# Feed-forward opening, decay expansion and second-half product order of a hybrid decoder layer

## What is computed

```python
z = h @ w_in                                    # all head groups from one projection
log_a = log_sigmoid((a_low @ w_gate_up + b_gate)) / GLA_TAU      # a_low has 16 columns
y_gla = rms_norm(gla_chunked(q, k, v, log_a)) * silu(g)
y_conv = c_b * causal_short_conv(c_c * c_h, conv_w)
y_xa = memory_cross_attention(xq, mk, mv)
mix = concatenate([y_gla, y_conv, y_xa]) @ w_out
x = layer_norm(alpha * x + mix, ln1_g, ln1_b)
ff = square(relu(x @ w_ff1)) @ w_ff2            # 1024 -> 4096 -> 1024
x = layer_norm(alpha * x + ff, ln2_g, ln2_b)
```

## Time and profile before

| | |
|---|---|
| median of three runs | 2171.8 us (2170.22 to 2173.83) |
| the profiled execution | 2171.97 us, of which the span from the first to the last instruction is 2170.3 us |
| PE busy | 2082.6 us (96%) |
| DVE busy | 1389.6 us (64%) |
| ACT busy | 1006.3 us (46%) |
| POOL busy | 516.7 us (24%) |
| mean granted TensorE clock | 0.987 of 2.4 GHz |

### The profile page before, as it was taken

The page is one execution under the profiler, slowest core; times in us unless marked ns, Lnnn a source line. Parts: engine busy times, 40 slices in busy tenths (PEclk is TensorE's granted clock), DMA queues, the critical chain, the costliest instruction groups (busy, mean ns, idle before and its releaser), DMA issues.

```text
span 2170.3 us, 28904 instructions
## 1 busy us (share of the span) xinstructions
PE 2082.6 (96%) x11392; PEld 1685.1 (78%) x11392; DVE 1389.6 (64%) x1898; ACT 1006.3 (46%) x1344; POOL 516.7 (24%) x483
## 2 busy tenths in 40 slices
PE   7999999999999999799999999999999999999996
PEld 5677787778777777688888788888788888788884
DVE  3668566756765687656556776666665645954458
ACT  3535454444444445545445654544433333633334
POOL 3002001101110213011000244444684700810004
PEclk9999999999999999899999999999999999999998
DMA  6222333324242514255646778777968665665563
GB/s 196 59 59 88 107 95 121 107 78 143 72 127 59 175 53 134 87 189 196 221 153 218 270 256 285 248 272 271 333 203 284 196 193 187 222 224 194 193 194 136
DMA packets 241063, 374.26 MB, mean 172 GB/s; under 512 B 16368, under 2 KB 117776, under 8 KB 240928
## 3 DMA queue, kind: packets, MB, share of 16 engines
q1 hardware_dynamic: 212096, 272.68, 38.6%
q0 software_dynamic: 28832, 99.74, 13.3%
HBM read 272.74 MB, written 99.61 MB: 172 GB/s over the span
## 4 chain that ended last, share of the span: by engine, by line
PE 51%; DVE 6%; ACT 2%; DMA 2%; issue 1%; POOL 0%; SPq 0%; DVEq 0%; ACTq 0%; POOLq 0%
PE main L68 9%; PE main L70 9%; PE main L69 9%; PE sc L68 6%; PE sc L69 6%; PE sc L70 6%; DVE w_lo L1563 3%; PE aux L70 1%; PE ob L70 1%; PE ob L68 1%; PE aux L68 1%; PE ob L69 1%; PE aux L69 1%; DMA w_b<-in_w_ff_dram 1%; DMA x_piece<-normed_dram 1%
## 5 line engine op out<-in xcount | busy, mean ns | idle before, releaser
L1563 DVE TENSOR_TENSOR w_lo<-w_b,w_hi 128x1024 fp32r<-128x1024 f32 x144 | 217.5, 1513 | 241.5 <-ACT w_hi L1533 241.5
L1563 DVE TENSOR_TENSOR w_lo<-raw,w_hi 128x1024 fp32r<-128x1024 f32 x144 | 205.5, 1430 | 128.6 <-ACT w_hi L1533 128.6
L1533 ACT ACTIVATE w_hi<-raw 128x1024 fp32r<-128x1024 f32 x144 | 152.5, 1060 | 256.7 <-PE main L70 112.6
L1533 ACT ACTIVATE w_hi<-w_b 128x1024 fp32r<-128x1024 f32 x144 | 152.2, 1057 | 176.9 <-PE aux L70 81.3
L1053 DVE TENSOR_TENSOR w_lo<-raw,w_hi 128x1024 fp32r<-128x1024 f32 x116 | 140.9, 1222 | 140.4 <-ACT w_hi L763 139.6
L68 PE MATMUL main<-xT_lo,w_hi 128*128 128x512 f32 (+1 forms) x528 | 217.2, 411 | 1.5 <-DVE xT_lo L1065 1.5
L69 PE MATMUL main<-xT_hi,w_lo 128*128 128x512 f32 (+1 forms) x528 | 205.5, 389 | 0.0
L70 PE MATMUL main<-xT_hi,w_hi 128*128 128x512 f32 (+1 forms) x528 | 205.4, 389 | 0.0
L68 PE MATMUL sc<-x_lo,w_hi 128*128 128x512 f32 x448 | 175.6, 392 | 8.4 <-DVE x_lo L1506 6.1
L68 PE MATMUL main<-x_lo,w_hi 128*128 128x512 f32 x448 | 175.7, 392 | 8.0 <-ACT z L1884 8.0
L68 PE MATMUL main<-w_lo,w_hi 128*128 128x512 f32 x448 | 175.8, 392 | 5.1 <-DVE w_lo L1563 5.0
(11 more groups left out here) (254 smaller groups left out, 4664.7 us busy)
## 6 DMA issues: line engine op xcount, KB each, us to landing
raw<-in_w_in_dram SPq DMA_DIRECT2D x80, 512.0 KB, 3.7
h_dram<-z SPq DMA_DIRECT2D x64, 512.0 KB, 3.9
raw<-h_dram SPq DMA_DIRECT2D x112, 256.0 KB, 2.7
w_b<-h_dram SPq DMA_DIRECT2D x112, 256.0 KB, 2.7
h_dram<-h_s SPq DMA_DIRECT2D x48, 512.0 KB, 4.0
rows<-in_x_dram POOLq DMA_DIRECT2D x32, 512.0 KB, 4.9
raw<-in_w_out_dram SPq DMA_DIRECT2D x32, 512.0 KB, 3.7
raw<-in_w_ff_dram SPq DMA_DIRECT2D x32, 512.0 KB, 6.7
```

Source lines behind the costliest of these rows:

```text
L1533: act.activation(ff.w_hi[:, n % RING, :], slot_tile(ff, m), ACT.Copy).then_inc(ff.hi_done, 1)
L1563: dve.tensor_tensor(ff.w_lo[:, n % RING, :], slot_tile(ff, m), ff.w_hi[:, n % RING, :].bitcast(F32), ALU.subtract).then_inc(ff.lo_done, 1)
```

## The change

Five things change.

1. **Decay expansion.** The low-rank value has 96 rows (hi, lo of the weight, three times) and is kept in fp32r: ACT copies all 96, DVE then subtracts in rows 64 to 95 to get the low part there. `w_gate` holds the matching six copies of the 16 rows, one pair of them as a low part. The two matmuls a block are fp32r, 96 rows deep. At the start six copies of `w_gate_up` are loaded instead of two, and ACT and DVE prepare the tiles in eight small instructions instead of two.
2. **Opening.** `x_high` and `x_low` are split into part 0 (three raw quarters, ready with the evacuation) and part 1 (four sums). Two of the four emptying instructions of the left half move ahead of the split of slot 6, the other two behind the sums of step 3. The splits of step q follow its own sums at once. The first product waits for part 0 of step 7 only, and product 1 for part 1. Slot splits 0 and 1 move back behind steps 5 and 7. The transposes of step 8 move from chunk 0 to chunk 1.
3. **Chunk 0.** ACT normalises two row tiles between snapshots 0 and 1 and two between 1 and 2. The tiles `z22` and `z12` change places with `h_s1` and `h_s4`, so that the snapshots wait for no store; DVE waits for the stores before it writes `h_s1` and `h_s4`. DVE forms the sum for slot 4 before the statistics.
4. **Second half.** The sequence is 5, 0, 1, 2, 3, 4, 6, so tiles 0 to 3 are complete after product 3. Products 4 and 6 then use the same banks back to back: the last two slots of product 4 run tile by tile (`BY_TILE`), and each bank is emptied before product 6 starts on it. Tiles 0 to 3 are finished during product 4, entirely by DVE in two passes, `(x - mean) * gain` (1024 wide) and `* rstd + bias` (two of 512), with ACT computing rstd only. POOL only stores them.
5. **Tail.** The last eight slots run tile by tile; four of them are held in memory of `acc0`, which the first half no longer needs. Tiles 4 to 7 are finished one by one behind their matmuls in the same two passes and stored in halves of 512 columns.

The diff, cut to its core:

```diff
@@ tiles
-            ff.z22, ff.z12, ff.z21 = (expand_sb(name, [P, 2, 512]) for name in ("z22", "z12", "z21"))
+            ff.h_s4, ff.h_s1, ff.z21 = (expand_sb(name, [P, 2, 512]) for name in ("h_s4", "h_s1", "z21"))
...
-            ff.h_s1, ff.h_s2 = (expand_sb(name, [P, 2, 512]) for name in ("h_s1", "h_s2"))
+            ff.z22, ff.h_s2 = (expand_sb(name, [P, 2, 512]) for name in ("z22", "h_s2"))
...
-            ff.h_s4 = expand_sb("h_s4", [P, 2, 512])
+            ff.z12 = expand_sb("z12", [P, 2, 512])
...
-        low = sb("low", [P, KT, 2 * RANK], F32R)
-        w_gate = sb("w_gate", [2 * RANK, 256])
+        low = sb("low", [P, KT, 6 * RANK], F32R)
+        w_gate = sb("w_gate", [6 * RANK, 256], F32R)
@@ mixer: POOL, ACT and DVE
-                             (w_gate[0:RANK, :], w_gate_up[0]),
-                             (w_gate[RANK:2 * RANK, :], w_gate_up[0]),
+                             *((w_gate_raw[RANK * i:RANK * i + RANK, :], w_gate_up[0]) for i in range(6)),
...
-                act.activation(lowT, aux[0:2 * RANK, :], ACT.Copy).then_inc(aux_free, 1)
+                act.activation(lowT, aux[0:6 * RANK, :], ACT.Copy).then_inc(gate_hi, 1)
...
+                dve.wait_ge(gate_hi, t + 1)
+                dve.tensor_tensor(lowT[64:96, :], aux[64:96, :], lowT[64:96, :].bitcast(F32), ALU.subtract
+                                  ).then_inc(aux_free, 1)
@@ x_evacuate, x_high
-        act.wait_ge(ff.x_lo_done, q if q >= 7 else q - 1)
+        act.wait_ge(ff.x_lo_done, 2 * (q if q >= 7 else q - 1))
...
+    if part == 0:
+        act.wait_ge(ff.x_evac, 2 * q + 2)
+    else:
+        act.wait_ge(ff.x_sum, 4 * q + 4)
     if q >= 6:
-        act.wait_ge(ff.x_lo_done, 6)
+        act.wait_ge(ff.x_lo_done, 2 * 6)
@@ slots
+SEQUENCE = [[0, 1, 2, 3, 4, 5, 6], [5, 0, 1, 2, 3, 4, 6]]
+SAME_TILE = [{3: 2, 4: 1, 5: 0}, {0: 5, 3: 2, 4: 1}]
+BY_TILE = 2
 TAIL = 4
-TAIL_K = 3
+TAIL_K = 8
+LAST_HELD = 2 * CONTRACT_SLOTS - TAIL_K
...
+    elif s >= LAST_HELD + 4:
+        act.wait_ge(ff.slot_used, m - 7)
+    elif s >= LAST_HELD:
+        act.wait_ge(ff.out_stored[s - LAST_HELD], 16)
     else:
         act.wait_ge(ff.slot_used, m - 3)
@@ PE
                 if m == 0:
-                    pe.wait_ge(ff.x_lo_done, X_STEPS)
+                    pe.wait_ge(ff.x_lo_done, 2 * X_STEPS - 1)
+                elif m == 1:
+                    pe.wait_ge(ff.x_lo_done, 2 * X_STEPS)
...
+                    if hf == 1 and p == 6 and k == 0:
+                        pe.wait_ge(fo_free, 4 * place(hf, p) - 4 + t + 1)
                     ins = piece(hf, p, k, t)
@@ ACT
-            if chunk == 0:
-                if i > 0:
-                    act.wait_ge(ff.stored[i], 16 * (HALF_CHUNKS // 2))
-            else:
+            if chunk > 0:
...
+        def inverse_deviation(c):
+            act.wait_ge(ln_stats, NT + c + 1)
+            act.activation(rstd[:, c:c + 1], mvar[:, c, 1:2], ACT.Ln, bias=eps_ln[:, :]).then_inc(ln_step, 1)
+            act.wait_ge(ln_step, 3 * NT + 2 * c + 1)
+            act.activation(rstd[:, c:c + 1], rstd[:, c:c + 1], ACT.Exp, scale=-0.5).then_inc(ln_step, 1)
...
+            if hf == 1 and at == 5 and k in (1, 4, 7, 10):
+                inverse_deviation(k // 3)
@@ DVE
+            elif p in (1, 3):
+                dve.wait_ge(ff.stored[{1: 2, 3: 1}[p]], 16 * (HALF_CHUNKS // 2))
...
+        def centred(c, step):
+            dve.wait_ge(ln_stats, NT + c + 1)
+            dve.scalar_tensor_tensor(out=acc[1][:, c, :], in0=acc[1][:, c, :], scalar=nmean[:, c:c + 1],
+                                     in1=g2_row[:, :], op0=ALU.add, op1=ALU.mult).then_inc(step, 1)
+
+        def scaled(c, step, n, ready):
+            dve.wait_ge(step, n)
+            dve.wait_ge(ln_step, 3 * NT + 2 * c + 2)
+            for d in range(2):
+                cols = slice(512 * d, 512 * d + 512)
+                dve.scalar_tensor_tensor(out=acc[1][:, c, cols], in0=acc[1][:, c, cols], scalar=rstd[:, c:c + 1],
+                                         in1=b2_row[:, cols], op0=ALU.mult, op1=ALU.add).then_inc(ready, 1)
...
+            if hf == 1 and at == 5 and k == KF - BY_TILE:
+                for t in range(4):
+                    if t < 3:
+                        dve.wait_ge(by_tile, t + 1)
+                    else:
+                        dve.wait_ge(slot_used, product_done(1, 4))
+                    add(1, 4, t)
```

More of the change, by code:

```diff
@@ L997, in _ @@
             split(0, 3)
[L998 to L999 removed]
+            act.wait_ge(small_landed, 16 * 11)
+            for i in range(3):
+                act.activation(low[:, :, 2 * RANK * i:2 * RANK * i + RANK], low_raw, ACT.Copy).then_inc(low_hi_done, 1)
+            act.activation(w_gate[:, :], w_gate_raw, ACT.Copy).then_inc(low_hi_done, 1)
             for i in range(4):
@@ L1687, in _ @@
                     sp.wait_ge(h_stored[p], 16 * CHUNKS)
-            for p in range(PRODUCTS):
+            for p in SEQUENCE[hf]:
                 for k in range(KF):
@@ new lines, in scaled @@
+        def scaled(c, step, n, ready):
+            dve.wait_ge(step, n)
+            dve.wait_ge(ln_step, 3 * NT + 2 * c + 2)
+            for d in range(2):
+                cols = slice(512 * d, 512 * d + 512)
+                dve.scalar_tensor_tensor(out=acc[1][:, c, cols], in0=acc[1][:, c, cols], scalar=rstd[:, c:c + 1],
+                                         in1=b2_row[:, cols], op0=ALU.mult, op1=ALU.add).then_inc(ready, 1)
+        for s in range(2 * CONTRACT_SLOTS):
+            hf, at, k = s // CONTRACT_SLOTS, s // KF % PRODUCTS, s % KF
+            if k == 0 and s > 0 and not (hf == 1 and at == 6):
+                h0, p0 = (hf, SEQUENCE[hf][at - 1]) if at else (hf - 1, SEQUENCE[hf - 1][6])
+                dve.wait_ge(slot_used, product_done(h0, p0))
+                for t in range(4):
+                    add(h0, p0, t)
+            if hf == 1 and at == 5 and k == KF - BY_TILE:
+                for t in range(4):
+                    if t < 3:
+                        dve.wait_ge(by_tile, t + 1)
+                    else:
+                        dve.wait_ge(slot_used, product_done(1, 4))
+                    add(1, 4, t)
+            if s + 4 < 2 * CONTRACT_SLOTS:
+                slot_low(dve, ff, EXPAND_SLOTS + s + 4)
+            if hf == 1 and at == 0 and 2 <= k < 10:
+                statistics(0, k - 2, 28)
+            if hf == 1 and at == 5 and 1 <= k < 13:
+                c = (k - 1) // 3
+                if k % 3 == 1:
+                    statistics(1, c, 48)
+                elif k % 3 == 2:
+                    if c == 0:
+                        dve.wait_ge(row_landed, 16 * 4)
+                    centred(c, head_step)
+                else:
+                    scaled(c, head_step, c + 1, head_ready)
+            if hf == 1 and at == 6 and k < 4:
+                half_statistics(1, TAIL + k, 1, 52)
```

292 lines of the change are left out of this document (161 added, 131 removed).

## The result

The changed kernel takes 2128.3 us (median of four runs, 2126.3 to 2131.0) against 2172.5 us for the kernel before on the same chip, 44 us less by the medians. Forecast were 2135.0 us, a gain of 37 us, in a range of 2128 to 2146 us, so the direction was right and the median lies just inside the range. The same kernel was timed once more later, beside other runs of before, and gave 0.9837 (0.9824 to 0.9851): 35 us by the ratio, 36.6 us by the medians. The profiled execution has a span of 2127.7 us where before had 2170.3 us, 42.6 us less.

A forecast was written before the change was run, and what follows sets the result against it. PE, busy for 96% of the span, was taken to bound the kernel. Gains of 19 + 8 - 0.5 + 3.5 + 7.1 = 37.1 us off 2171.97 us gave 2135 us, range 2128 to 2146 us for 8 in 10.

The forecast's parts named there:

- Opening: Up to product 4 of chunk 0: PE's waits go or shrink, 19 us gained, bounds 12 and 23.5 us.
- Forecast waits of 2.5 and 0.7 us: Chunk 0, before products 3 and 4: PE still waits 2.5 and 0.7 us for snapshots 1 and 2.
- allowance: Up to product 4 of chunk 0: 19 us taken instead of 20.4 us, for semaphores or a slower clock.
- waits found again between 930 and 1030 us: Sign of being wrong: the same waits a chunk later, where six steps of x operands fall in three chunks.
- Decay: Eight decay matmuls in the mixer: 1.02 us saved on each, 8 us taken, bounds 5.4 and 8.2 us.
- start-up: Start of the kernel: more DMA issues and small instructions for the decay tiles cost 0.5 us, bounds 0 and 2 us.
- Second half: From product 4 of the second half to the last slot: net gain 3.5 us, bounds 0 and 5.4 us.
- both terms: Last products of the second half: 5.4 us of wait and clock gained, 1.9 us lost to a new wait.
- the new wait: Before product 6's first matmul in the second half: PE waits about 2 us because DVE reaches the four adds late.
- End: Behind the last matmul: 7.5 us instead of 14.6 us, gain 7.1 us, bounds 6 and 8 us.

The follow-up runs named there:

- The additional run: The changed kernel with the last four slots by tile instead of eight (TAIL_K = 4); ratio to the kernel before 0.9846 (0.9831 to 0.9860).

## Why the prediction was right

- **Opening: right, and its marks hold.** No wait at the right-hand pieces. The stretch from the start of the projection to the first product was counted as 882.5 - 831.7 = 50.8 us and took 51.1 us. Forecast waits of 2.5 and 0.7 us before products 3 and 4 came out as 1.86 and 0.19 us. The count by hand gave 20.4 us; taking 19 for allowance was the only error, 1.8 us. Two steps in it were judged wrongly in their weight: letting the first product go with part 0 alone is worth nothing once the row tiles are next (run with the coarser wait, in which the splits themselves stay in two parts), and moving step 8, which got no term, guards some 4 us of the gain (4.87 us wait without it). One of the prediction's signs of being wrong, waits found again between 930 and 1030 us, did show in small: the waits for row pieces, 1.03 and 0.58 us before, are 2.69 us at 966.43 us and 1.09 us at 1007.62 us.
- **Decay: right.** 1.01 us a matmul by the starts (660.96 to 662.67 us before, and 652.49 to 653.19 us after, 1.71 less 0.70), so 8.1 us; with start-up 7.5 us between the means of all mixers. The Trainium skill (FP8 and Floating Point Precision, TensorE Precision Notes) has four passes for a true fp32 matmul, which would save 0.68 us each; the rows have 1.01 us, so by them the old one held PE for 0.23 + 1.01 = 1.24 us. The 10.6 us of the one pair hold 3 us of chance.
- **Second half: the net, 3.7 for 3.5 us, was right by luck, since both terms were too small.** The prediction took DVE's first addition, 2106.91 us, for the end of product 5. PE's first matmul of product 6 starts at 2104.42 us; the addition stood behind a slot split. So product 6 took 51.1 us and lost 7.6 us, not 5.4. On the other side the new wait was 1.90 us as forecast, with groups of 9.2 us (9.3 forecast), but it came at the last two slots of product 4, for a slot split, not before product 6 for the emptied bank, and in this profile cost 1.6 us more by the clock, which six of the seven other profiles with this wait don't show. 7.6 less 1.9 and 1.6 is 4.1; 3.7 was measured. In the later run of the same kernel the stretch takes 310.4 us: 5.3 us gained.
- **End: right.** 7.51 us from the start of the last matmul, 7.5 forecast; the gain is 7.5 and not 7.1 us because the prediction counted the 14.6 us of before from DVE's addition and not from the matmul (14.97 us). The additional run shows why: 4.53 us of DVE a tile must fit into the PE time of a tile.
- **What no term held:** 2.8 us lost in the expansion and 2.7 us won at the start of the contraction. The loss is no chance: it is in all nine profiles that have both the new mixer and the whole new opening, and in none of the four without one of the two. PE's waits for row pieces, which grew from 1.6 to 3.8 us, make up 2 us of it; they are 3.5 to 3.8 us in those nine, 1.8 us with the opening alone and 2.1 us with the mixer alone. Which transfer is in the way there stays open. The contraction's first stretch depends on slot loads and took 47.5 to 51.8 us up to the first addition in the profiles, so this part of the pair is chance. That the two cancel is luck.
- The gain beyond the forecast, 5.5 us in the pair of spans, is thus 3.1 us of chance in the mixer, 1.8 us of needless allowance, and 0.6 us of the rest. By the ratios the two timings of the changed kernel gave 40.6 and 35.4 us, one above the forecast of 37.1 and one below it.

## What to carry to other kernels

Count a queue forward by hand from measured durations and trust the count: in the opening the marks came out within 1 us, and the allowance for unknowns was the error. Take a product's end from PE's rows, never from the engine that empties its bank. Look where an engine holds back another by a small step in front of the work that it is waited for: moving two tiny ACT instructions by one slot took 1 us off each group and a wait of 1.9 us off PE. And read an edit worth less than the spread of the whole from its own stage, once you know how far that stage spreads between profiles of unchanged code: the first half of the contraction, some 310 us with loads in it, differed by 4.6 us between profiles here.

## What the runs showed of the hardware

- A pass of DVE with two SBUF sources (128x1024, fp32) takes 1.23 us alone, 3.38 us beside two-source passes of POOL, and 1.23 to 2.11 us beside one-source passes (2.77 us each), which hold it back in their first 0.88 us only. DVE's additions from PSUM aren't touched (0.68 us).
- The clock behind a wait of PE isn't the same each time. Behind 1.90 us at one place it fell in two of eight profiles (0.66 in a 5 us window); the same kernel is once among the two and once among the six in which it stayed at 1.00. Behind the 2.5 to 2.8 us waits for a row piece at about 970 us it fell in two of nine (the runs with four row tiles and with four slots by tile). Behind 5.90 us (0.51) and 8.04 us it fell.
- A plain fp32 matmul of 32x128 by 32x512 held PE for 1.24 us, an fp32r one of 96x128 by 96x512 for 0.23 us.
- The same mixer took 820.5 to 826.8 us in eleven profiles. This spread alone is as large as most terms of the change.
